# Inversion inside a gated delta rule: 32x32 block transposes on VectorE, level masks applied to the product, and narrow weight columns as the stationary operand

## The reference

```python
# block 1: 8 columns of w_in are forget logits, one for each head
log_f = jax.nn.log_sigmoid(fl + forget_b)
cum = jnp.cumsum(log_f, axis=1)
# block 2: 16 columns of gdn_w_in are the decay and the beta of each head
beta = jax.nn.sigmoid(b_in)
g = -jnp.exp(a_log) * jax.nn.softplus(a_in + dt_bias)
# in chunks of tokens, for each head:
G = jnp.cumsum(g, axis=-1)
a_low = jnp.where(strict, beta[..., None] * kk * decay_mat, 0.0)
sol = lax.linalg.triangular_solve(a_low + eye, rhs, left_side=True, lower=True, unit_diagonal=True)
```

## Time and profile before

| | us |
|---|---|
| median of 3 runs | 1403.87 |
| lowest and highest | 1403.49, 1406.48 |
| the profiled execution | 1401.33 |
| its span in the trace | 1399.2 |

### The profile page before, as it was taken

The page is one execution under the profiler, slowest core; times in us unless marked ns, Lnnn a source line. Parts: engine busy times, 40 slices in busy tenths (PEclk is TensorE's granted clock), DMA queues, the critical chain, the costliest instruction groups (busy, mean ns, idle before and its releaser), DMA issues.

```text
span 1399.2 us, 16562 instructions
## 1 busy us (share of the span) xinstructions
PE 1316.1 (94%) x6807; PEld 1114.9 (80%) x6807; DVE 757.2 (54%) x801; ACT 629.6 (45%) x756; POOL 100.9 (7%) x138
## 2 busy tenths in 40 slices
PE   8999999988999998999796999999988889999997
PEld 7888879886788886998696778888767777888886
DVE  5555447954655536478734455543656525554444
ACT  5444336634444424455532254442445644444423
POOL 0000001001000003001421100000101101000001
PEclk9999999999999998999999999999998999999999
DMA  8865537410765563544100276555364313765540
GB/s 276 255 186 191 195 123 231 155 42 30 229 186 187 180 210 113 159 153 164 31 1 0 59 233 201 191 172 204 111 205 151 106 61 111 227 199 179 185 144 30
DMA packets 140139, 212.27 MB, mean 152 GB/s; under 512 B 10233, under 2 KB 101245, under 8 KB 140060
## 3 DMA queue, kind: packets, MB, share of 16 engines
q1 hardware_dynamic: 140064, 211.22, 46.8%
HBM read 210.14 MB, written 1.05 MB: 151 GB/s over the span
## 4 chain that ended last, share of the span: by engine, by line
PE 87%; DVE 6%; ACT 3%; issue 2%; POOL 0%; DMA 0%; SPq 0%; ACTq 0%; DVEq 0%
PE bank L1400 25%; PE bank L1402 25%; PE bank L1401 25%; PE bank L1423 2%; PE bank L1765 1%; DVE wlo L938 1%; PE bank L1516 1%; PE bank L1777 1%; PE bank L1631 1%; DVE xTlo L959 1%; ACT whi L372 1%; PE bank L1755 1%; DVE X L982 1%; ACT xThi L388 1%; PE bank L1700 0%
## 5 line engine op out<-in xcount | busy, mean ns | idle before, releaser
L938 DVE TENSOR_TENSOR wlo<-raw,whi 128x2048 fp32r<-128x2048 f32 x190 | 434.1, 2291 | 299.0 <-ACT whi L372 298.6
L372 ACT ACTIVATE whi<-raw 128x2048 fp32r<-128x2048 f32 x190 | 362.3, 1913 | 241.3 <-PE bank L1402 234.6
L1400 PE MATMUL bank<-whi,xThi 128*128 128x512 f32 x1024 | 412.7, 403 | 21.7 <-DVE xTlo L959 9.9
L1401 PE MATMUL bank<-wlo,xThi 128*128 128x512 f32 x1024 | 405.5, 396 | 0.0
L1402 PE MATMUL bank<-whi,xTlo 128*128 128x512 f32 x1024 | 405.2, 396 | 0.0
L1400 PEld LDWEIGHTS bank<-whi,xThi 128*128 128x128 f32 x1024 | 196.5, 192 | 68.3 <-DVE xTlo L959 11.2
L1402 PEld LDWEIGHTS bank<-whi,xTlo 128*128 128x128 f32 x1024 | 196.2, 192 | 42.7
L1401 PEld LDWEIGHTS bank<-wlo,xThi 128*128 128x128 f32 x1024 | 196.6, 192 | 39.6
L1400 PE MATMUL bank<-whi,hThi 128*128 128x512 f32 x352 | 139.9, 397 | 0.0
L1401 PE MATMUL bank<-wlo,hThi 128*128 128x512 f32 x352 | 138.9, 394 | 0.0
L1402 PE MATMUL bank<-whi,hTlo 128*128 128x512 f32 x352 | 138.8, 394 | 0.0
(11 more groups left out here) (337 smaller groups left out, 1342.0 us busy)
## 6 DMA issues: line engine op xcount, KB each, us to landing
raw<-in_ffn_w_dram SPq DMA_DIRECT2D x176, 256.0 KB, 4.1
...
```

What stands on the lines that cost most here:

```text
L372: act.activation(whi[w % SPLIT][:], raw[w % RAW][:], ACT.Copy).then_inc(w_hi, 1)
L938: dve.tensor_tensor(wlo[w % SPLIT][:], raw[w % RAW][:], whi[w % SPLIT][:].bitcast(F32), ALU.subtract).then_inc(w_lo, 1)
L1400: pe.matmul(psum, lhs[0], rhs[0], start=start, stop=False, skip_group_check=True)
L1401: pe.matmul(psum, lhs[0], rhs[1], start=False, stop=False, skip_group_check=True)
```

## The change

Inversion:

- The level masks go to the product. Y is made with the unmasked `A_[q]`, and VectorE multiplies it by `lvl[l - 1]` (now 128x64) while it empties PSUM. ScalarE's copies of Y and all `Lm` products of VectorE and GpSimd are gone, but for level 6, where ScalarE copies the lower half of Y.
- T is turned into U by VectorE's 32x32 block transpose, `dve.transpose`, one instruction for each unit (128x512) at levels 1 to 4; at level 5 it is two instructions that move one 32x128 block each. TensorE's transposes and ScalarE's copies of them are gone.
- Level 0 is, for each unit, a product with the mask `pair`, the addition of the identity, and a block transpose, all on VectorE and interleaved over the units.
- Level 6 takes 64 rows of `A_`, `T` and `U`, and 64 columns of U in place of 128.
- Buffers move: `QK[2]` and `QK[3]` take the place of `y4`, hence one new wait for `g_v` in the stage before the inversion. `Lm` is gone.

Narrow projections:

- `narrow_cols` takes the weight columns as the stationary operand, high and low parts side by side (16 or 32 columns), and 256 tokens as the moving one: 8 matmuls with both parts on the high part of the activations, 8 with the high part on the low one. Results lie in PSUM transposed. ScalarE copies them to SBUF, and two small float32 matmuls, `folded`, add the parts and turn them back.
- In `mixer1` `narrow_cols` stands before `block_cols(s + 2)`, `folded` where `narrow_rows` stood.
- In `mixer2` `narrow_cols` stands where `narrow_rows` stood; `folded` comes halfway through the second `block_rows`. VectorE's and ScalarE's work on the logits moves behind the gate `sg` of the first pair of slots. VectorE's is in a function `log_decay` with the same six instructions.
- GpSimd makes the two folding matrices at the start of the program (two memsets and four selects of at most 32x16), and fewer masks for the inversion. The rounding of the narrow weights is two instructions on each engine in place of one.

```diff
+        act.wait_ge(*once("m_flx"))
+        act.activation(flT[:], bank[6][0:2 * H1, 0:SEQ], ACT.Copy).then_inc(did("m_flT"), 1)
...
-        act.wait_ge(*once("g_z"))
-        act.activation(a_log[:], a_log[:], ACT.Exp)
-        step(act.activation(eab[:], eab[:], ACT.Exp))
-        act.activation(eab[:], eab[:], ACT.Ln, bias=1.0).then_inc(did("g_ln"), 1)
-
         for b in range(2):
             split(s + 2 * b + 1 + SPLIT)
             act.wait_ge(w_used, s + 2 * b + 2)
             for t in range(NT):
                 ins = act.activation(sg[:, t, b * 512:(b + 1) * 512], bank[2 * b + t][:], ACT.Silu)
             ins.then_inc(sem("g_gate"), 1)
+            if b == 0:
+                act.wait_ge(*once("g_abx"))
+                act.activation(abT, bank[7][0:4 * H2, 0:SEQ], ACT.Copy).then_inc(did("g_abT"), 1)
             split(s + 2 * b + 2 + SPLIT)
+            if b == 0:
+                act.wait_ge(*once("g_z"))
+                act.activation(a_log[:], a_log[:], ACT.Exp)
+                step(act.activation(eab[:], eab[:], ACT.Exp))
+                act.activation(eab[:], eab[:], ACT.Ln, bias=1.0).then_inc(did("g_ln"), 1)
...
-        for l in range(7):
-            if l:
-                for q in range(UNITS):
-                    act.wait_ge(sem("i_Y"), UNITS * (l - 1) + q + 1)
-                    act.activation(Y[q], bank[q][:, 0:256], ACT.Copy).then_inc(sem("i_Y_in"), 1)
-            if l < 6:
-                for q in range(UNITS):
-                    act.wait_ge(sem("i_TT"), UNITS * l + q + 1)
-                    act.activation((U[q] if l else T[q]).rearrange("p h c -> p (h c)"), bank[4 + q][:], ACT.Copy)\
-                        .then_inc(sem("i_U"), 1)
+        for q in range(UNITS):
+            act.wait_ge(sem("i_Y"), UNITS * 5 + q + 1)
+            act.activation(Y[q][64:], bank[q][64:, 0:256], ACT.Copy).then_inc(sem("i_Y6"), 1)
...
-        for l in range(7):
-            for q in range(HG, UNITS):
-                if l == 0:
-                    pool.wait_ge(sem("g_AQ"), 2 * q + 1)
-                elif l == 1:
-                    pool.wait_ge(sem("i_one"), q + 1)
-                else:
-                    pool.wait_ge(sem("i_Y"), UNITS * (l - 2) + q + 1)
-                pool.tensor_tensor(Lm[q], A_[q], lvl[:, l:l + 1, :].broadcast_to([P, 4, P]), ALU.mult)\
-                    .then_inc(sem("i_L1"), 1)
...
-        def level_mask(l):
-            for q in range(HG):
-                if l == 1:
-                    dve.wait_ge(sem("i_one"), q + 1)
-                elif l:
-                    dve.wait_ge(sem("i_Y"), UNITS * (l - 2) + q + 1)
-                dve.tensor_tensor(Lm[q], A_[q], lvl[:, l:l + 1, :].broadcast_to([P, 4, P]), ALU.mult)\
-                   .then_inc(sem("i_L0"), 1)
-
-        level_mask(0)
-        for q in range(UNITS):
-            dve.wait_ge(*((sem("i_L0"), q + 1) if q < HG else (sem("i_L1"), q - HG + 1)))
-            if q == 0:
-                dve.wait_ge(sem("g_bv"), UNITS)
-            dve.tensor_tensor(U[q], ident[:].unsqueeze(1).broadcast_to([P, 4, P]), Lm[q], ALU.subtract)\
-               .then_inc(sem("i_one"), 1)
-        level_mask(1)
+        for q in range(UNITS + 2):
+            if q < UNITS:
+                if q == 0:
+                    dve.wait_ge(sem("g_bv"), UNITS)
+                dve.tensor_tensor(U[q], A_[q], pair[:].unsqueeze(1).broadcast_to([P, 4, P]), ALU.mult)\
+                   .then_inc(sem("i_pair"), 1)
+            if 0 <= q - 1 < UNITS:
+                dve.wait_ge(sem("i_pair"), q)
+                dve.tensor_tensor(U[q - 1], U[q - 1], ident[:].unsqueeze(1).broadcast_to([P, 4, P]), ALU.add)\
+                   .then_inc(sem("i_one"), 1)
+            if 0 <= q - 2:
+                dve.wait_ge(sem("i_one"), q - 1)
+                dve.transpose(T[q - 2].rearrange("p h c -> p (h c)"), U[q - 2].rearrange("p h c -> p (h c)"))\
+                   .then_inc(sem("i_T0"), 1)
         for l in range(1, 6):
-            b = 2 ** l
-            level_mask(l + 1)
+            b, n = 2 ** l, UNITS * (l - 1)
             for q in range(UNITS):
-                v = T[q].rearrange("p h (i j) -> p (h i) j", j=2 * b)[:, :, 0:b]
-                dve.wait_ge(sem("i_Z"), UNITS * (l - 1) + q + 1)
-                dve.wait_ge(*((sem("i_U"), q + 1) if l == 1 else (sem("i_T"), UNITS * (l - 2) + q + 1)))
-                dve.tensor_tensor(v, v, bank[q][:, 256:512].rearrange("p (n j) -> p n j", j=b), ALU.subtract)\
-                   .then_inc(sem("i_T"), 1)
+                dve.wait_ge(sem("i_Y"), n + q + 1)
+                dve.tensor_tensor(Y[q].rearrange("p (h c) -> p h c", h=4), bank[q][:, 0:256].rearrange("p (h c) -> p h c", h=4),
+                                  lvl[:, l - 1:l, :].broadcast_to([P, 4, 64]), ALU.mult).then_inc(sem("i_Y_in"), 1)
+            for q in range(UNITS + 1):
+                if q < UNITS:
+                    v = T[q].rearrange("p h (i j) -> p (h i) j", j=2 * b)[:, :, 0:b]
+                    dve.wait_ge(sem("i_Z"), n + q + 1)
+                    dve.tensor_tensor(v, v, bank[q][:, 256:512].rearrange("p (n j) -> p n j", j=b), ALU.subtract)\
+                       .then_inc(sem("i_T"), 1)
+                if q:
+                    dve.wait_ge(sem("i_T"), n + q)
+                    if l < 5:
+                        ins = dve.transpose(U[q - 1].rearrange("p h c -> p (h c)"), T[q - 1].rearrange("p h c -> p (h c)"))
+                    else:
+                        for r in (0, 64):
+                            ins = dve.transpose(U[q - 1][r:r + 32, :, r + 32:r + 64], T[q - 1][r + 32:r + 64, :, r:r + 32])
+                    ins.then_inc(sem("i_U"), 1)
         for q in range(UNITS):
             dve.wait_ge(sem("i_Z"), UNITS * 5 + q + 1)
-            dve.tensor_tensor(U[q][0:64], U[q][0:64], bank[4 + q][0:64, :].rearrange("p (h c) -> p h c", h=4), ALU.subtract)\
+            dve.tensor_tensor(U[q][0:64, :, 64:], U[q][0:64, :, 64:], bank[4 + q][0:64, 0:256].rearrange("p (h c) -> p h c", h=4),
+                              ALU.subtract)\
...
-    def narrow_rows(psum, c0, n, src):
-
-        for t in range(NT):
-            for k in range(KD):
-                ins = passes(psum[:, t * n:(t + 1) * n], [x[:, k, t * P:(t + 1) * P] for x in src],
-                             [x[:, k, c0:c0 + n] for x in (narrow_hi, narrow_lo)], t == 0 and k == 0, k == KD - 1)
+    def narrow_cols(psum, weights, n):
+
+        for k in range(KD):
+            both = weights[:, k].rearrange("p i n -> p (i n)")
+            pe.matmul(psum[0:2 * n, 0:SEQ], both, xThi[:, k, :], start=k == 0, stop=False, skip_group_check=True)
+            ins = pe.matmul(psum[0:n, 0:SEQ], weights[:, k, 0, :], xTlo[:, k, :], start=False, stop=k == KD - 1,
+                            skip_group_check=True)
+        return ins
+
+    def folded(psum, at, both, fold, n):
+
+        for t in range(NT):
+            ins = pe.matmul(psum[:, at + t * n:at + (t + 1) * n], both[:, t * P:(t + 1) * P], fold[:], start=True, stop=True)
...
+        pe.wait_ge(*once("narrow_lo"))
+        narrow_cols(bank[6], narrow_m, H1).then_inc(did("m_flx"), 1)
...
-        pe.wait_ge(*once("narrow_lo"))
-        narrow_rows(bank[6], 0, H1, xT).then_inc(did("m_fl"), 1)
+        pe.wait_ge(*once("folds"))
+        pe.wait_ge(*once("m_flT"))
+        folded(bank[6], SEQ, flT, fold_m, H1).then_inc(did("m_fl"), 1)
         block_cols(s + 4, xT, [bank[4], bank[5]])
         pe.wait_ge(*once("m_lf"))
-        pe.matmul(bank[6][:, 32:32 + H1], upto[:], lf[:, 0, :], start=True, stop=True)
-        pe.matmul(bank[6][:, 32 + H1:32 + 2 * H1], ones[:], lf[:, 0, :], start=True, stop=False)
-        pe.matmul(bank[6][:, 32 + H1:32 + 2 * H1], upto[:], lf[:, 1, :], start=False, stop=True).then_inc(did("m_cum"), 1)
+        pe.matmul(bank[6][:, 288:288 + H1], upto[:], lf[:, 0, :], start=True, stop=True)
+        pe.matmul(bank[6][:, 288 + H1:288 + 2 * H1], ones[:], lf[:, 0, :], start=True, stop=False)
+        pe.matmul(bank[6][:, 288 + H1:288 + 2 * H1], upto[:], lf[:, 1, :], start=False, stop=True).then_inc(did("m_cum"), 1)
...
+
+        def gate_logits():
+            pe.wait_ge(*once("g_abT"))
+            folded(bank[7], SEQ, abT, fold_g, 2 * H2).then_inc(did("g_ab"), 1)
         for b in range(2):
             block_rows(s + 2 * b, xT, [bank[2 * b], bank[2 * b + 1]], k_ready=tile_ready("n4") if b == 0 else None,
-                       tilewise=b == 0)
+                       tilewise=b == 0, halfway=gate_logits if b else None)
             if b == 0:
-                narrow_rows(bank[7], H1, 2 * H2, xT).then_inc(did("g_ab"), 1)
+                narrow_cols(bank[7], narrow_g, 2 * H2).then_inc(did("g_abx"), 1)
 
         pe.wait_ge(*once("g_g"))
         for t in range(NT):
-            pe.matmul(bank[7][:, 64 + t * H2:64 + (t + 1) * H2], upto[:], gl[:, t, 0:H2], start=True, stop=True)
```

(35 more changed lines are left out.)

109 lines of the change are left out of this document (68 added, 41 removed).

## The result

| | median of the runs | ratio to before (95% interval) | profiled span | mean granted clock |
|---|---|---|---|---|
| before | 1403.68 us | 1 | 1399.2 us | 0.967 |
| after | 1419.88 us | 1.0119 (1.0101 to 1.0138) | 1418.2 us | 0.943 |

The change makes the kernel slower by 1.2%. I had forecast 1387.3 us and put 0.92 on faster. Rival C came true, to which I gave 0.02: the clock falls inside the inversion.

What follows compares the result with a forecast made beforehand. TensorE was taken to bound the inversion and `mixer2`'s narrow projection, VectorE to be tighter in `mixer1`; 9.1 + 0.3 + 6.2 + 1.0 = 16.6 us off gave 1384.7 profiled, 1387.3 by the runs' median, range 1383.5 to 1391.5.

Steps and rivals of the forecast that it cites:

- Rival C: Inversion: clock falls once the 128-column transposes are gone, 352 instructions cost 36 us, 1423 in all; chance 0.02.
- the term for the beginning: Start of inversion: VectorE alone does level 0, TensorE starts Y at 687.6, partly at half clock; 0.3 us gained.
- block transpose 128x512: Inversion, VectorE: one transpose takes 0.61 us, like a 128x512 product; bounds 0.36 and 2.28.
- a level, Y to Y: Inversion: TensorE keeps Y and Z, 64 instructions, 7.07 us a level, 1.77 less than before.
- inversion, first mask to recurrence: Whole inversion: 9.1 us gained from levels 1 to 6 and 0.3 at its beginning.
- `mixer2`: Narrow projection of `mixer2`: 6.2 us gained on TensorE, no clock fall, log decays ready with 2.0 us of cover.
- `mixer1`: Narrow projection of `mixer1`: first row maximum unmoved, earlier exponentials gain 1.0 us, between 0 and 1.9.
- A: Inversion: block transpose about twice as dear, 1.22 us, VectorE bounds the levels; about 1392 us; chance 0.10.
- B: Inversion: block transpose four times as dear, 2.28 us, a level 12.0 us on VectorE; 1418 us; chance 0.04.
- F: Inversion: levels bound by latency from engine to engine, nothing gained there; 1396.7 us; chance 0.03.
- rival D: `mixer2`: log decays come late, TensorE waits 2 to 4 us; 1391 us; chance 0.07.
- Rival E: `mixer1` gives back all of TensorE's 6.2 us; 1382 us; chance 0.05.

Runs made afterwards that it cites:

- the kernel with one group of transposes ahead: Changed kernel plus 16 transposes of 128 columns of a constant ahead of level 1's first product, none later: 1393.8 us.
- the wide kernel: Changed kernel whose products Y move all 128 columns of T, VectorE reading the used half: 1380.7 us, 0.9831 of before.

## Why the prediction was wrong

**The step that failed** is the argument against rival C: "the 7.10 us from 698.99 hold nothing but 64-column matmuls and stay at 1.00, as in every level". The row is right, and proves only that 64-column work keeps the clock for 7.10 us between two groups of 16 transposes. I read it as if it said that 64-column work can run at full clock without them. The change removed the very groups that bounded that stretch, so no row of before showed its state after. The row that spoke was in the same group: the first 3.39 us at 0.55 and 1.00 behind, with 16 transposes between. I saw the rise, and gave it to the time that passed, not to what ran in it: the term for the beginning has Y0 and Y1 "at half clock" and "Y2 and Y3 at full clock". That is the first thing that failed. In the changed kernel the clock never rose, through 78 us of such products, while in the kernel with one group of transposes ahead they kept it for 36 us. And in `mixer2` I had noted that the clock fell 4.5 us into narrow matmuls without a gap, so the trace of before already had a stretch in which a busy TensorE lost it. Rival C's price was good: 36 us of 352 instructions, 1423; measured 1419.9.

The Trainium skill (TensorE: Matmul & The Clock Gate, Part 1) says that throttled is the default and that activity releases it. The traces agree where the activity is of 128 columns (one group ahead: up 3.1 us after it starts). A busy row alone didn't do it: 78 us without a gap ran at 0.50.

**The other terms**, by the kernels in which they can be read:

| term | forecast | measured |
|---|---|---|
| block transpose 128x512 | 0.61 us (0.36 to 2.28) | 0.70, 0.60 to 0.63 from start to start |
| a level, Y to Y | 7.1 | 13.65 at half clock; 7.14 in the wide kernel |
| inversion, first mask to recurrence | -9.4 | +24.9; -10.7 in the wide kernel (47.99) |
| level 6 and the wait behind it | 7.8 | 11.2 at half clock; 6.3 in the wide kernel (718.93 to 725.27) |
| T0 ready after the first mask | 3.7 | 3.9 (675.67 to 679.54) |
| T1 behind T0 | 1.3 | 1.8: three operations stand between the two transposes, not two |
| `mixer2` | -6.2 | -6.0 (555.35 to 568.85, 13.50, against 19.50) |
| `mixer1` | -1.0 (0 to -1.9) | about -1.8 |

*The inversion's order of work* was foreseen: the transpose costs one pass, TensorE is the bound of the levels, VectorE has slack (busy 28.59 of 40.27 us at full clock), and rivals A, B and F are out. With the clock up the part gains 10.7, although its first 3.85 us of TensorE work are at half clock. It is more than the forecast 9.4 because of level 6: its last 32 instructions, with 64 stationary columns, start 0.061 us apart, and I had priced them like the others.

*`mixer2`.* 16 narrow matmuls take 1.82, `folded` 0.54, no half clock behind them, and the sums stand at 568.85 with no wait. The log decays had 2.6 us of cover, and rival D is out.

*`mixer1`.* The first row maximum comes at 276.57, 0.90 earlier than in before, but the narrow matmuls start 0.95 earlier too than the product that stood there (218.26 against 219.21), an offset from ahead of the change: it stands where it stood, as said. TensorE idles 6.7 us (I had 7 to 8), and the clock is 0.50 behind it:

```profile
PE bank L1656 <- ACT p L531: 6.7, 1, 6.7
```
```profile
278.50:282.00 3.50, 3.50 (x15) 3.22 (x14) 3.50 (x11) 1.47 (x7) 0.00 (x0) 0.50 0.84 269
283.00:286.50 3.50, 3.50 (x30) 3.45 (x30) 2.10 (x6) 1.30 (x5) 0.00 (x0) 0.96 0.00 0
```

It is up again at 283.3, sooner than in before (286.1), so that nearly all of the possible 1.9 is kept: TensorE's next weight slot starts at 315.26 against 317.99, 2.7 us earlier, 0.95 of it the offset. Rival E is out.

Had I weighed C by what the rows really bound (no row of before without the transposes, one row in which the clock rises while they run), I would put it at a third or more by my own judgement, and the range would have reached 1423.
